# Expert-value product: 512 columns of value rows behind each load of activations

## The reference

```
a = jax.nn.gelu(jnp.einsum('thkd,td->thk', u_sel, hb), approximate=False)
v_sel = jnp.take(v, idx, axis=0)
return jnp.einsum('thk,thkd->td', (g * a).astype(hb.dtype), v_sel)
```

## Time and profile before

| | us |
|---|---|
| median of 3 runs | 3401.7 |
| lowest and highest run | 3396.45, 3410.36 |
| span of the profiled execution | 3397.2 |
| expert-value product in it, first matmul start to last | 1326.2 to 2026.8 |
| PE busy over the span | 3362.4 (99%) |
| DVE busy | 2500.3 (74%) |
| ACT busy | 1963.3 (58%) |

### The profile page before, as it was taken

One profiled execution on the slowest core, in us unless ns is written; L12 is line 12 of the kernel. 1 busy time (PEld: TensorE's weight loads), 2 busy tenths in 40 slices (PEclk: granted clock), 3 DMA queues, 4 the chain that ended last, 5 costly groups with the idle time before them and its releaser, 6 DMA issues.

```text
span 3397.2 us, 80038 instructions
## 1 busy us (share of the span) xinstructions
PE 3362.4 (99%) x29184; PEld 3319.9 (98%) x29184; DVE 2500.3 (74%) x4438; ACT 1963.3 (58%) x3483; POOL 736.1 (22%) x709
## 2 busy tenths in 40 slices
PE   8999999999999999999999999999999999999999
PEld 7999999999999999999999998999999999999999
DVE  7886688788875555676788879998667776666555
ACT  5456655677765555555555556765565665555554
POOL 1001130377777723555000000000000000000000
PEclk9999999999999999999999999999999999999999
DMA  8867788577777766877898864545555555555555
GB/s 325 335 221 253 248 299 303 161 187 190 186 193 194 194 204 225 271 244 249 320 341 338 335 218 132 176 160 183 162 189 192 187 190 192 192 191 196 187 192 179
DMA packets 234085, 758.61 MB, mean 223 GB/s; under 512 B 60072, under 2 KB 63664, under 8 KB 221104
## 3 DMA queue, kind: packets, MB, share of 16 engines
q1 hardware_dynamic: 167328, 608.57, 52.8%
q0 software_dynamic: 62624, 139.63, 15.0%
q10 hardware_dynamic: 3952, 7.91, 0.7%
HBM read 732.78 MB, written 21.11 MB: 222 GB/s over the span
## 4 chain that ended last, share of the span: by engine, by line
PE 94%; DVE 4%; ACT 1%; issue 1%; DMA 1%; DVEq 0%; SPq 0%; ACTq 0%
PE PS L502 24%; PE PS L508 23%; PE PS L507 23%; PE PS L651 7%; PE PS L661 7%; PE PS L659 7%; DVE wlo L1701 1%; DVE big L1695 0%; PE PS L934 0%; DMA raw<-peer_v_dram 0%; PE PS L761 0%; DVE big L1628 0%; PE PS L923 0%; PE PS L880 0%; PE PS L946 0%
## 5 line engine op out<-in xcount | busy, mean ns | idle before, releaser
L1061 ACT ACTIVATE whi<-raw 128x512 fp32r<-128x512 f32 x1864 | 1157.8, 630 | 1022.8 <-PE PS L508 652.3
L1557 DVE TENSOR_TENSOR wlo<-raw,whi 128x512 fp32r<-128x512 f32 x1480 | 1024.9, 706 | 605.9 <-ACT whi L1061 585.6
L502 PE MATMUL PS<-tok_parts_hi,whi 128*128 128x256 f32 x2048 | 569.4, 278 | 0.8 <-ACT big L1286 0.7
L508 PE MATMUL PS<-tok_parts_hi,wlo 128*128 128x256 f32 x2048 | 568.3, 277 | 0.0
L651 PE MATMUL PS<-whi,ev_parts_hi 128*128 128x256 f32 x2032 | 561.8, 276 | 1.1 <-DVE wlo L1557 1.1
L661 PE MATMUL PS<-whi,ev_parts_lo 128*128 128x256 f32 x2032 | 562.1, 277 | 0.0
L507 PE MATMUL PS<-tok_parts_lo,whi 128*128 128x256 f32 x2030 | 561.7, 277 | 0.0
L659 PE MATMUL PS<-wlo,ev_parts_hi 128*128 128x256 f32 x2026 | 559.9, 276 | 0.0
L1701 DVE TENSOR_TENSOR wlo<-raw,whi 128x512 fp32r<-128x512 f32 x564 | 381.6, 695 | 129.2 <-ACT whi L1150 84.1
L434 POOL DMA_INDIRECT gates_dram<-big x256 | 427.0, 1668 | 200.2 <-issue 91.1
L1150 ACT ACTIVATE whi<-raw 128x512 fp32r<-128x512 f32 x436 | 271.4, 629 | 250.4 <-PE PS L508 247.5
(11 more groups left out here) (552 smaller groups left out, 8201.3 us busy)
## 6 DMA issues: line engine op xcount, KB each, us to landing
raw<-peer_u_dram SPq DMA_DIRECT2D x256, 512.0 KB
raw<-peer_v_dram SPq DMA_DIRECT2D x256, 512.0 KB
raw<-w_in_dram SPq DMA_DIRECT2D x240, 512.0 KB
big<-w_mod_dram POOLq DMA_DIRECT2D x96, 1024.0 KB, 6.6
raw<-w_up_dram SPq DMA_DIRECT2D x176, 512.0 KB
raw<-w_down_dram SPq DMA_DIRECT2D x88, 512.0 KB
raw<-w_out_dram SPq DMA_DIRECT2D x64, 512.0 KB
gates_dram<-late POOLq DMA_DIRECT2D x16, 1024.0 KB, 9.0
```

The source lines that it names most:

```text
L502: pe.matmul(out, hi, rhi, start=start, stop=False, **more)
L508: return pe.matmul(out, lo, rhi, start=False, stop=stop, **more)
L1061: f(whi[:, m % PAIRS, quarter(q)], raw[:, m % RING, quarter(q)], ACT.Copy).then_inc(hi_ready, 1)
L1557: dv.tensor_tensor(wlo[:, m % PAIRS, quarter(q)], raw[:, m % RING, quarter(q)], whi[:, m % PAIRS, quarter(q)], ALU.subtract).then_inc(lo_r ...
```

## The change

The two sides of a bank become one matmul of 512 columns. For each quarter and each set of tokens there are now three matmuls, high by high, high by low, low by high, where there were six. A matmul that opens a bank has `start` set where the first of the two sides had it. The cut matmuls are gone, and with them the bodies written out between the loops: turn 0 is written out and turns 1 to 31 are one loop. The waits on `lo_ready`, `stage_lo` and `banks_free` and the count of `quarters_used` stand where they stood. No other engine's instructions change.

```diff
-            def spread_tokens(name, turns, staged, cuts):
+            def spread_tokens(name, turns, staged):
...
-                                    for side in range(2):
-                                        bank = PS[:, t * 4 + half * 2 + q, side * SEQ:(side + 1) * SEQ]
-                                        at_ = slice((2 * q + side) * SEQ, (2 * q + side + 1) * SEQ)
-                                        pe.matmul(bank, e_hi[:, o_], whi[:, half, at_], start=opens and side == 0,
-                                                  stop=False, skip_group_check=True)
-                                        if cut and b == 1 and half == 0 and q == 1 and t == 0 and side == 0:
-                                            for part in (slice(0, CUT), slice(CUT, SEQ)):
-                                                pe.matmul(bank[:, part], e_hi[:, o_],
-                                                          wlo[:, half, (2 * q + side) * SEQ + part.start:(2 * q + side) * SEQ + part.stop],
-                                                          start=False, stop=False, skip_group_check=True)
-                                        else:
-                                            pe.matmul(bank, e_hi[:, o_], wlo[:, half, at_], start=False, stop=False,
-                                                      skip_group_check=True)
-                                        last = pe.matmul(bank, e_lo[:, o_], whi[:, half, at_], start=False,
-                                                         stop=False, skip_group_check=True)
+                                    bank = PS[:, t * 4 + half * 2 + q, :]
+                                    pe.matmul(bank, e_hi[:, o_], whi[:, half, quarter(q)], start=opens, stop=False,
+                                              skip_group_check=True)
+                                    pe.matmul(bank, e_hi[:, o_], wlo[:, half, quarter(q)], start=False, stop=False,
+                                              skip_group_check=True)
+                                    last = pe.matmul(bank, e_lo[:, o_], whi[:, half, quarter(q)], start=False, stop=False,
+                                                     skip_group_check=True)
                                 last.then_inc(quarters_used, 1)
...
-                for at, until in zip((0,) + cuts, cuts + (turns,)):
-                    if at:
-                        body(at, False, True)
-                    with pe.Fori(at + 1, until) as g:
-                        body(g, False)
+                with pe.Fori(1, turns) as g:
+                    body(g, False)
...
-            spread_tokens("peer_v", N_SUB // 4, 0, (2, 10, 15, 17, 22, 26))
+            spread_tokens("peer_v", N_SUB // 4, 0)
```

More of the change, by code:

```diff
@@ L630, in spread, with body @@
                     body(g, False, False)
-            def spread_tokens(name, turns, staged, cuts):
+            def spread_tokens(name, turns, staged):
                 h0_ = FIRST[name]
-                def body(g, opening, cut=False):
+                def body(g, opening):
                     for b in range(4):
```

## The result

| | before | after |
|---|---|---|
| median, runs | 3399.9 us, 7 | 3415.4 us, 7 |
| lowest and highest run | 3396.5, 3410.4 | 3412.8, 3419.7 |
| ratio of the times | | 1.0045, 95% interval 1.0034 to 1.0055 |
| span of the profiled execution | 3397.2 | 3418.0 |
| product, first matmul start to last | 1326.2 to 2026.8 | 1330.8 to 2047.4 |

The change makes the kernel slower by 0.45%. 3378.5 was forecast, at most 3394. That is just under the 0.5% which the prediction took for the least that a measurement of this kernel can tell, but the interval of the ratio doesn't reach 1, so the loss is real.

A forecast was written before the change was run, and what follows sets the result against it. The prediction took PE's matmul pace in the expert-value product as the bound. Savings of 20.5 us from pace, 0.7 from cuts and 2.0 from the opening pace made 23.2, from median 3401.7 to 3378.5 us; range 3363 to 3394.

The forecast's parts named there:

- What bounds the kernel: Expert-value product: PE is busy throughout, so a change in its matmuls' pace moves the end one for one.
- The pace of 512 columns: Expert-value product: 220.0 ns per matmul, so 3072 take 675.8 us in place of 696.3, 20.5 us saved.
- opening pace: Expert-value product, first matmul to first cut: 117.8 ns steps, read as late weight loads; 2.0 us saved when gone.
- Cuts: Expert-value product: six matmuls cut in two cost 0.11 us each; removing them saves 0.7 us.
- Stalls: Expert-value product: two stalls near 1625, after a burst of modulation-weight transfers, stay at 1.6 us.
- Rival 1: Expert-value product: the extra 6.67 ns belongs to weight handover and is hidden; 215.7 ns a matmul, 3365; chance 0.15.
- Rival 2: Expert-value product: opening pace is a clash of two reads and lasts; 4.4 to 6 ns per matmul, 3392 to 3397; chance 0.20.
- Rival 3: Expert-value product, 1660 to 1960: transfers set the pace, those 300 us don't shrink, stalls are added; 3388; chance 0.10.
- Rival 4: Expert-value product: 512 columns go as two halves, each at the opening pace; 235.6 ns a matmul, 3426; chance 0.08.

The follow-up runs named there:

- distance 0: The changed kernel with the activations' tiles at byte offset 0 instead of 64, so load and stream addresses agree modulo 256: 3393.3 us, ratio 0.9979 to before.
- the run with widths: The changed kernel with each bank of 512 columns streamed whole or in two parts of various widths, turn by turn: 3521.9 us in all.
- the kernel with offsets 64 to 160: The changed kernel with four activation tiles instead of two, at byte offsets 64, 96, 128 and 160, one for each step of a turn: 3418.7 us.
- `passes`: Turns 13 to 16 of the changed kernel with reordered matmuls, 256-column halves next to each other within a pass: 235.5 ns per 512 columns; whole run 3419.6 us.

## Why the prediction was wrong, point by point

- **What bounds the kernel:** right. The pace of these matmuls moved the end one for one: 15.9 us in the product, 0.2 behind it.
- **The pace of 512 columns:** this is the step that failed. From 258 columns at 120.0 ns I made a rule, columns in pieces of 16 and one piece for each matmul, and took 220.0. Measured: 233.3, so 716.8 for 3072 instead of 675.8, 41 us on one term and 20.5 saved turned into 20.5 lost. The rule was made from two widths, 256 and 258, and I took the 6.7 ns on top for a fixed price. It is 20.0 ns at 512 columns here. Of the 13.3 too little, 6.7 depend on where load and stream lie: with 512 columns it is 13.3 ns on top at distance 0 and 20.0 at 64, which is the place that suits 256 columns. The other 6.7 are there at distance 0 too, and what they are stays open. The row of 256 columns may also have said little of a stream's own price: in the run with widths, parts of 16 to 240 columns behind a full load start 108 to 114 ns behind each other whatever their width (the first in each three of the narrower ones aside), and 113.3 stands right beside that. A bound existed that would have held: the earlier trace rows put twice the opening pace at 235.6, and I took it for the unlikely end.
- **Cuts:** 0.7 us was their price in time, and my sum took it back. It was not their worth. Without them the kernel of 256 columns has a median of 3419 instead of 3400. With 512 columns there is nothing for them to do, so leaving them out was harmless.
- **The opening pace:** I read 2.0 us as a late load that vanishes with longer streams. It is a state at 256 columns, and was short only because a cut came: without the cut it went on for 112 us more, until a hiccup. The sum got 2.0 us for it, and they were gained, since no separate pace shows at 512; but the whole product pays 6.7 ns a matmul above what distance 0 gives.
- **Stalls:** 1.6 us were to stay, none is there. Each quarter lasts 1.40 us instead of 1.36 and ACT's waits for memory fell to 7.0 us. That the slower pace is the reason isn't shown: the kernel with offsets 64 to 160 is as slow and has PE waiting three times at 1658 to 1666, 2.1 us in all, and the two executions at distance 0 lost no more than 0.2 and 0.5 us behind the burst.
- **Rival 1** (215.7 ns, 3365) fell. The rule of the Trainium skill beside it (TensorE: Matmul & The Clock Gate, Back-to-back issue gap) would give 215.8; no 512-column stretch in any run went below 226.7.
- **Rival 2** came nearest in kind: it had the two reads in each other's way, and half of the miss does hang on the distance between them. Its price was too small: 4.4 to 6 ns above 220, from streams of 256 and 272 columns, and 13.3 were measured. That the opening pace is the same thing is not shown, since both paces of 256 columns occur at one distance. The rule of the Trainium skill that spoke against it (same page, Step-by-step: what each phase is for: reads have ports of their own, a load does not slow a running matmul) is not borne out in its second half: 6.7 ns a matmul hang on the address of the load. Of the ports no run here tells anything.
- **Rival 3** (transfers) fell: PE waited for nothing.
- **Rival 4** came out nearest (235.6 a matmul, 3426) with the wrong reason. 512 columns don't go as two halves: at distance 0 512 columns take 226.7 where two halves take 240.0, and at 64 they take 233.3 where two halves take 235.5 or 226.7.
- **The range** left out rival 4 and the dearer half of rival 2. No row from which a price of 512 columns was made was wider than 272, and the range was drawn tight around the middle one.

## What to carry to other kernels

When a change swaps the widths of loads and streams, the byte offset of the two tiles modulo 256 is worth trying again: here one number was worth 20 us, and made a loss of 0.45% a gain of 0.2%. A step per matmul read at one width is no price for another width; cost it from both sides and let the range hold both. Before a small oddity such as a cut matmul is taken out, ask which state of the engine it ends, since its worth doesn't show in a profile in which it is there.

## What the runs showed of the hardware

- At 512 columns of F32R a matmul takes 226.7 to 227.5 ns with load and stream within 16 bytes modulo 256, 228.9 to 229.6 at 192, 232.1 to 234.0 at -32 and at 32 to 160. At distance 64 the order of the matmuls changes nothing, and a cut only costs its 0.1 us. A cause (say, that both reads meet in the same part of the memory) was not shown; only the dependence was.
- At 256 columns the same operands have two paces, 113.3 and 117.8 ns, in one and the same kernel, and changed from the slower to the quicker at a hiccup of 0.3 us or a cut; in another order of the matmuls (`passes`) a stall didn't bring the change. 512 columns kept within 1.3 ns at each distance, and no stall or cut changed their pace.
- Behind a full load, matmuls of 16, 64 and 128 columns start 0.11 us apart whatever their width, but for the first step in each three (0.03 to 0.06 us).
- At distance 0 a load of 32 columns makes the matmul 5 ns slower than a load of 128.
